# Dense stages of a two-block forward pass, from full fp32 products to three products of split high and low parts

## The reference

```python
def first_block(...):                      # DEPTH 2
    for i in range(2):
        sh1, sc1, g1, sh2, sc2, g2 = split(silu(c) @ ada_w[i] + ada_b[i], 6)  # 12 "rotations" of 1024 columns in all
        u = layer_norm(h) * (1 + sc1) + sh1
        if i == 0:
            uc = modulated layer_norm(ctx)                   # 256 context tokens
            p = u @ w_in                                     # 3072 columns: conv gates, q | k, v
            kv of the context = uc @ w_in[:, K0:]
            y = concat(conv_mixer, diff_attention) @ w_out_mix
        else:
            y = fourier_mix(u) @ w_out_fourier
        h = post_norm(h, g1 * y)
        h = post_norm(h, g2 * (relu(mod(h) @ mlp_w1)**2 @ mlp_w2))   # 1024 -> 4096 -> 1024
def second_block(...):
    h += fox_attention(rms_norm(h))        # fox_w_in 4 x 1024 columns, fox_w_out
    h += hier_moe(...)                     # 32 experts, 12 MB of weights for each pair of experts
    h += retention(rms_norm(h))            # ret_w_in 6 x 1024 columns, ret_w_out 2048 -> 1024
    h += hier_moe(...)
    return rms_norm(h)
```

## Time and profile before

| | us |
|---|---|
| median of 3 runs (2267.81 to 2272.15) | 2269.62 |
| the profiled execution, its own time | 2266.69 |
| its span, first to last instruction | 2264.9 |
| TensorE busy | 2138.2 |
| VectorE busy | 860.4 |
| ScalarE busy | 606.4 |

### The profile page before, as it was taken

How to read it: one execution, slowest core, us unless ns; L and a number is a source line. 1 busy time by engine, 2 the same in 40 slices (tenths; PEclk the granted TensorE clock), 3 DMA queues, 4 the chain that set the end, 5 groups by cost and what they waited for, 6 DMA issues and landing times.

```text
span 2264.9 us, 34188 instructions
## 1 busy us (share of the span) xinstructions
PE 2138.2 (94%) x13808; PEld 1421.8 (63%) x13809; DVE 860.4 (38%) x1536; ACT 606.4 (27%) x913; POOL 37.0 (2%) x38
## 2 busy tenths in 40 slices
PE   7998899999999997889999999989999899999998
PEld 5746777887888786754444444478887444444444
DVE  3765567653664664241111111156343111111112
ACT  1113366332673454211111111044411111111101
POOL 0000100000100200000000000000000000000000
PEclk9998999999999999989999999989998999999999
DMA  9950277822455255079999999825642799999994
GB/s 381 383 193 2 97 244 251 301 84 75 149 186 186 82 189 213 17 306 388 410 410 410 410 410 410 353 82 196 228 168 83 295 410 409 410 410 410 410 410 192
DMA packets 157222, 603.00 MB, mean 266 GB/s; under 512 B 10063, under 2 KB 10501, under 8 KB 157141
## 3 DMA queue, kind: packets, MB, share of 16 engines
q1 hardware_dynamic: 156544, 601.33, 69.4%
q0 software_dynamic: 320, 0.39, 0.1%
q10 hardware_dynamic: 276, 0.13, 0.0%
HBM read 600.73 MB, written 1.05 MB: 266 GB/s over the span
## 4 chain that ended last, share of the span: by engine, by line
PE 71%; SPq 10%; DMA 8%; ACT 4%; DVE 4%; issue 3%; DVEq 0%; ACTq 0%
PE bank L907 12%; PE bank L547 12%; SPq L421 9%; PE bank L525 7%; PE bank L919 6%; PE bank L548 6%; DMA expert_w<-in_expert_w_gu 5%; PE bank L891 4%; PE bank L584 4%; PE bank L938 4%; PE bank L566 3%; PE bank L674 1%; PE bank L673 1%; DMA u<-in_ada_w 1%; DMA dense_w<-in_ada_w 1%
## 5 line engine op out<-in xcount | busy, mean ns | idle before, releaser
L907 PE MATMUL bank<-expert_w,work 128*32 128x512 f32 (+1 forms) x4032 | 453.1, 597 | 26.8 <-issue 12.2
L907 PEld LDWEIGHTS bank<-expert_w,work 128*32 128x32 f32 (+1 forms) x4032 | 132.5, 111 | 345.9 <-issue 313.0
L395 DVE TENSOR_TENSOR w_low<-dense_w,w_high 128x2048 fp32r<-128x2048 f32 x96 | 219.4, 2291 | 172.5 <-ACT w_high L388 171.8
L388 ACT ACTIVATE w_high<-dense_w 128x2048 fp32r<-128x2048 f32 x104 | 197.5, 1911 | 265.2 <-DMA dense_w<-in_mlp_w 179.6
L919 PE MATMUL bank<-expert_w,work 128*32 128x512 f32 (+1 forms) x2016 | 226.4, 594 | 0.0
L1940 DVE TENSOR_TENSOR work<-work,bank 128x512 f32<-128x512 f32 x32 | 22.0, 688 | 410.1 <-ACT work L1324 410.1
L547 PE MATMUL bank<-hidden_pairs,w_high 128*128 128x512 f32 x496 | 174.5, 396 | 2.7 <-DVE expert_w L1452 2.7
L547 PE MATMUL bank<-u_pairs_mlp,w_high 128*128 128x512 f32 x448 | 164.5, 404 | 11.9 <-ACT u_pairs_mlp L1110 5.9
L919 PEld LDWEIGHTS bank<-expert_w,work 128*32 128x32 f32 (+1 forms) x2016 | 63.5, 110 | 144.4 <-issue 144.4
L547 PE MATMUL bank<-u_pairs,w_high 128*128 128x512 f32 x392 | 143.2, 403 | 6.4 <-DVE u_pairs L1434 5.4
L891 PEld LDWEIGHTS bank<-work 128*128 128x128 f32 x1088 | 125.9, 194 | 32.2 <-issue 32.1
(11 more groups left out here) (332 smaller groups left out, 2619.3 us busy)
## 6 DMA issues: line engine op xcount, KB each, us to landing
expert_w<-in_expert_w_gu SPq DMA_DIRECT2D x256, 1024.0 KB, 18.1
expert_w<-in_expert_w_down SPq DMA_DIRECT2D x128, 1024.0 KB, 16.7
dense_w<-in_mlp_w SPq DMA_DIRECT2D x64, 1024.0 KB, 5.2
dense_w<-in_ret_w_in SPq DMA_DIRECT2D x24, 1024.0 KB, 5.2
u<-in_ada_w SPq DMA_DIRECT2D x40, 512.0 KB, 6.3
work<-in_ada_w SPq DMA_DIRECT2D x40, 512.0 KB, 6.1
dense_w<-in_fox_w_in SPq DMA_DIRECT2D x16, 1024.0 KB, 5.2
dense_w<-in_w_in SPq DMA_DIRECT2D x12, 1024.0 KB, 8.3
```

Source lines behind the costliest of these rows:

```text
L388: nc.scalar.activation(w_high[:, at % RING], dense_w[:, at % RING], ACT.Copy, scale=scale).then_inc(S("w_high_ready"), 1)
L395: ins = nc.vector.tensor_tensor(w_low[:, at % RING], dense_w[:, at % RING], high, ALU.subtract)
L907: last = mm(free[half][cols, :], rows[:, k, cols], pieces[:, k, a, half * 512:(half + 1) * 512], start=k == 0, stop=k == KT - 1)
```

## The change

All dense stages use `by_rows` with split chunks and three products of 256 columns (keys and values, and the value blocks, 512): high by high, low weights by high, high weights by low. Each tile has one sum, evacuated by one engine (ScalarE for `w1`, with Relu, fox q, k and g, with Sigmoid for g, ret q, k and g, with Silu for g); `upper` and `sum_of` go. The activations of `w_in`, `mix`, `fourier`, `fox_out` and `ret_out` are split as well: high part on ScalarE, low part on VectorE, 256 columns at a time. For `w_in`, `fox_out` and `ret_out` there are only two places for high parts of chunks, so that a split waits until the chunk two before it is used. The context is loaded right behind x and normalised and turned before rotation 1; chunk (0, 0) of `w_in` is moved ahead of the last two ada chunks in the ring. Rotations 2 to 5 stay in the `w_in` stretch (pieces 0 to 31, two a chunk at first), 6 to 11 (48 pieces) are summed in the first MLP. The folds move: 6, 7 after the first MLP, 8, 9 after the next norm, 10, 11 after `post1_1`, in the place of warming products. GpSimd's loads wait for `mod_ready`. The last four pieces of the second expert stage's first pair are loaded after `ret_out` and not after the group norm's variance.

```diff
-                   ... ("ada_0", 4), ("z", 4), ("ada_1", 4), ("w_in", 8), ("zc", 4), ("w_in_1", 8) ...
+                   ... ("ada_0", 4), ("zc", 4), ("z", 4), ("ada_1", 4), ("w_in", 8), ("w_in_1", 8) ...
+        for table in (CHUNKS, SOURCE, LAST_TILE, USED, SPLIT_NO):
+            table.insert(6, table.pop(8))
+        HIGH_OF, WAS, holds = [], [], {}
+        for at, (name, i, j) in enumerate(CHUNKS):
+            where = {"w_in": (w_high, (4 * i + j) % 2), "fox_out": (w_high_fox, j % 2), "ret_out": (w_high_ret, (4 * i + j) % 2)}.get(
+                name, (w_high, at % RING))
+            key = (name if name in ("fox_out", "ret_out") else "", where[1])
+            HIGH_OF.append(where[0][:, where[1]])
+            WAS.append(holds.get(key) if name != "ada" and at - holds.get(key, 0) < RING else None)
...
         def split_high(act, at, scale=1.0):
             wait_chunk(act, at)
-            nc.scalar.activation(w_high[:, at % RING], dense_w[:, at % RING], ACT.Copy, scale=scale).then_inc(S("w_high_ready"), 1)
+            if WAS[at] is not None:
+                wait_used(act, WAS[at])
+            nc.scalar.activation(HIGH_OF[at], dense_w[:, at % RING], ACT.Copy, scale=scale).then_inc(S("w_high_ready"), 1)
...
+            sp.dma_start(ctx_tok, A["ctx"][0].rearrange("(t p) d -> p t d", p=P)).then_inc(S("in_ctx"), 16)
+            for at in range(chunk("w_in", 1, 0)):
                 load(at)
             sp.dma_start(const[:, N_FIRST:], A["consts"][:, N_FIRST:]).then_inc(S("in_const_rest"), 16)
+            for q in range(4):
+                load_ada(q)
+            q = 4
             for n, at in enumerate(range(chunk("w_in", 1, 0), chunk("w1_0", 0, 0))):
-                for q in range(4 * n, 4 * n + 4):
-                    load_ada(q)
                 load(at)
+                for _ in range(2 if n < 6 else 4):
+                    if q < 32:
+                        load_ada(q)
+                        q += 1
...
+            def columns(high, low):
+                def piece(out, n, k, w, w_rest, start, stop):
+                    c = slice(n * P, (n + 1) * P)
+                    mm(out[:, 0:SEQ], w[:, c], high[:, k, :], start=start, stop=False)
+                    mm(out[:, 0:SEQ], w_rest[:, c], high[:, k, :], start=False, stop=False)
+                    return mm(out[:, 0:SEQ], w[:, c], low[:, k, :], start=False, stop=stop)
+                return piece
...  # TensorE: the start
             ada(0)
-            pe.wait_ge(S("z_ready"), TT)
+            pe.wait_ge(S("z_ready"), 2 * TT)
+            turn("zc", ctx_tok)
             turn("z", z_tok)
             ada(1)
...  # VectorE: w_in, twelve steps
+            for step in range(3 * RING):
+                if 1 <= step < 3 * RING - 1:
+                    split("w_in", (step + 1) // RING, (step + 1) % RING)
+                if step == 0:
+                    ... modulate the context ...
+                if step == 1:
+                    ... low parts of the context ...
+                if step == 8:
+                    ... rope_q()
+                if step >= 8:
+                    conv(step - 8)
+                for q in range(2 * step, 2 * step + 2) if step < 8 else range(4 * step - 16, 4 * step - 12):
                     add_ada(q)
...  # VectorE: end of the first attention
+                if step == 4:
+                    split("mix", 0, 0)
+                    for n in range(4):
+                        low_of_cat(n)
+                    split("mix", 0, 1)
+                    low_of_cat(4)
+                    low_of_cat(5)
...  # ScalarE: ret_out
+            for n in range(2 * KT):
+                if n % 2 == 0:
+                    c = n // 2 + 1
+                    if c < 2 * RING:
+                        split("ret_out", c // RING, c % RING)
+                act.wait_ge(S("ret_gated"), n + 1)
+                fn(rgate_high[:, n, :], rgate[:, n, :], ACT.Copy).then_inc(S("rgate_high"), 1)
...  # VectorE: ret_out, for each head hd
+                for n in range(4 * hd, 4 * hd + 4):
+                    low_in_place(rgate_low[:, n, :], rgate[:, n, :], rgate_high[:, n, :], "rgate_high", n + 1, "rgate_low")
+                    if n % 2:
+                        c = n // 2 + 1
+                        if c < 2 * RING:
+                            split("ret_out", c // RING, c % RING)
...  # TensorE: ret_out
+                by_rows("ret_out", g, TILES["ret_out"], 8, columns(rgate_high[:, eight], rgate_low[:, eight]),
+                        lambda j: pe.wait_ge(S("rgate_low"), KT * g + 2 * j + 2), g == 0, g == 1)
```

More of the change, by code:

```diff
@@ L81 @@
 ADA_PE = 2
-ADA_HEAD = 8
+ADA_HEAD = 6
 HALVES = 4
+ADA_AT = {}
+for _x in range(24):
+    ADA_AT.setdefault(2 + 2 * _x // 3, []).append(32 + _x)
+for _x in range(24):
+    ADA_AT.setdefault(18 + 7 * _x // 12, []).append(56 + _x)
 ATTN = []
@@ new lines, in tokens, with piece @@
+            def tokens(high, low):
+                def piece(out, n, k, w, w_rest, start, stop):
+                    rows, c = slice(n // 2 * P, (n // 2 + 1) * P), slice((n % 2) * 512, (n % 2 + 1) * 512)
+                    mm(out[:, :], high[:, k, rows], w[:, c], start=start, stop=False)
+                    mm(out[:, :], high[:, k, rows], w_rest[:, c], start=False, stop=False)
+                    return mm(out[:, :], low[:, k, rows], w[:, c], start=False, stop=stop)
+                return piece
@@ L573, in pairs_of, with halves @@
+            def halves(where, k0=0):
+                x = pairs[where][:, k0:k0 + KT]
+                return x[:, :, HIGH, :], x[:, :, LOW, :]
             def pairs_of(name):
@@ L1211, in _ @@
                     deviation(sub_rstd[g % 2], T0 + diff_tile(g, 7), 1)
+                if step == 4:
+                    split("mix", 0, 1)
+                    high_of_head(0)
+                    high_of_head(1)
+                if step == 5:
+                    split("mix", 0, 2)
+                    high_of_head(2)
+            split("mix", 0, 3)
+            high_of_head(3)
             def mlp(l):
@@ L1306, in _ @@
                         copy_out(t, fpT[:, a, :], bank(t)[:, 0:384])
+                if step >= 2:
+                    high_of_gated(step - 2)
+            high_of_gated(FOX_HEADS // 2 - 1)
+            for j in (2, 3):
+                split("fox_out", 0, j)
             def experts(l):
@@ L1655, in _, with residual @@
                                            ALU.mult, ALU.mult).then_inc(S("sub_out"), 1)
-                if 1 <= step <= 3:
+                if 1 <= step <= 2:
                     for r in (2 * step, 2 * step + 1):
                         take_fold(T0 + ATTN.index(("f", r)), r)
-            def residual(name, l, gate, halves):
+                if step == 4:
+                    split("mix", 0, 0)
+                    for n in range(4):
+                        low_of_cat(n)
+                    split("mix", 0, 1)
+                    low_of_cat(4)
+                    low_of_cat(5)
+                if step == 5:
+                    split("mix", 0, 2)
+                    low_of_cat(6)
+            split("mix", 0, 3)
+            low_of_cat(7)
+            def residual(name, l, gate):
                 link(V.tensor_scalar(resid, h[:, :, :], ALPHA, None, ALU.mult))
@@ L1784, in _ @@
                     wait_tile(dve, t)
-                    dve.wait_ge(S("fox_gate"), g + 1)
+                    wait_evac(dve, TILES["fox_g"] + g)
                     evac(V.tensor_tensor(fgate[:, g, :], fgate[:, g, :], bank(t)[:, 0:SEQ], ALU.mult), t)
+                if step >= 2:
+                    low_of_gated(step - 2)
+            low_of_gated(FOX_HEADS // 2 - 1)
+            for j in (2, 3):
+                split("fox_out", 0, j)
             def add_to_h(name):
```

423 lines of the change are left out of this document (198 added, 225 removed).

## The result

The changed kernel takes 2287.1 us (median of 5 runs, 2284.3 to 2291.4), the kernel before 2270.0 beside it: ratio 1.0074, 95% interval 1.0058 to 1.0090. So it is slower by 17 us; 2260 was predicted, in a range that ended at 2282. The profiled execution has a span of 2286.8 against 2264.9, 21.9 more, at a mean granted clock of 0.965 against 0.974.

A forecast was written before the change was run, and what follows sets the result against it. Outside the expert stages TensorE's products were taken to bound the kernel, inside them the weights' transfers after some ten pairs. The terms summed to -7 us, so 2260 us was forecast, in a range of 2236 to 2282.

The forecast's parts named there:

- I take 0.116, so 0.348: Dense stages: a split product of 256 columns priced at 0.116 us, three in a row at 0.348.
- rival 3: Dense stages: three products of 256 cost 0.361, not 0.348, by a fixed 13 ns each; 2285 us; chance 17%.
- The two-in-a-row places: Sixteen tile closes in the earlier trace with two 256-column products in a row, 0.115 us each, taken as the price's model.
- The pair's remainder, 0.120: Upper bound for a 256-column product: pair of 0.347 less 0.2268 for 512 columns, so 0.361 us for three.
- w2 over 90.5 (pitch): Sign that would show the forecast wrong: the w2 stage taking over 90.5 us, by its product pitch.
- The start: Start and w_in: -5 us, bounds -14 to +3, with TensorE idle about 11 us before chunk (0, 2).
- Attention and `mix`: Attention and mix: 0 net, 5.3 us saved in products against a later mix start; bounds -4 to +3.
- First MLP -9.5: First MLP: -9.5 us, as one evacuation per tile takes VectorE out of the block boundaries; bounds -12 to +3.
- The fourth rival: First MLP: VectorE's queue at 90% and pieces ahead of chunks hold the loads; +12 on its term, 2272; chance 8%.
- Fourier, second MLP, `fox_in`, `ret_in`, `fox_out`: Later dense stages: Fourier -5.8 us, second MLP -1, fox_in and ret_in -0.5 each, fox_out -5.3.
- `ret_out` +17.5: ret_out: products give back 10.7 us, six gaps of 3.3 cost 20, lost clock 8; bounds +9 to +22.
- The rule on weight loads: TensorE: if loads overlapped products only across differing row groups, the change would lose some hundreds of us; given 1 in 100.

The follow-up runs named there:

- e3: Changed kernel with second-MLP product widths altered (384, 128 columns; values wrong), read for pitches alone: a triple of 384 columns takes 0.52 us, of 128 takes 0.33.
- e2: Changed kernel with w_in (0, 0) put back behind the last two ada rotation 1 chunks in the load order; ratio 1.0024 to the kernel before.
- e6: e2 with ada rotation 1 copies ahead of the split of w_in (0, 0), and the split of (0, 1) behind all x parts; ratio 1.0019 to before.
- e4: Changed kernel with w1 and w2 of both MLPs back as pairs of 512 and 256 columns; ratio 1.0129 to the kernel before.
- e1: Changed kernel with ScalarE's ret_out split of the next chunk behind the high parts of the current chunk's two tiles; ratio 1.0015 to the kernel before.
- e9: Changed kernel with ScalarE's and VectorE's ret_out lists reordered, e6's start orders, and VectorE's mix split and low parts made earlier; ratio 0.9860 to before.
- e8: Changed kernel with w2 of both MLPs and q, k blocks of fox_in and ret_in back as pairs; ratio 1.0100 to the kernel before.
- e12: e10 with w2 of both MLPs as pairs, w1 as triples; ratio 0.9815 to the kernel before.
- e10: e9 with TensorE making ada rotation 1 before turning context and x, and ScalarE's rotation 0 copies ahead of the context's squares; ratio 0.9821 to before.

## Why the prediction was wrong

- **The price of three products: the step that failed most.** "I take 0.116, so 0.348", and rival 3, at 17%, had 0.361. Measured 0.360. 0.012 on each of 1920 triples is 23 of the 29 us by which the span missed (-7 forecast, +21.9 measured); with that term alone put right the forecast would have been 2283. The two-in-a-row places looked like the very thing, but they stood between 512-column products, and there a single spacing is no price: over before's w2_1 a 256-column product starts 0.232 after a wide one and the next wide one 0.115 after it, 0.348 in sum. The pair's remainder, 0.120, came from a steady stream and was right. The 13 ns stand at 256, 384 (e3) and 512 columns, so the rival's mechanism holds at 256 columns. The prediction's own sign, "w2 over 90.5 (pitch)", came out at 92.3.
- **The start: the wait foreseen, its place in time not.** TensorE idle 11 us before (0, 2), by VectorE's split behind the additions: 11.37, q 0 added at 76.35 and the split after it. But (0, 2) starts at 81.2 where the forecast has 71.7, and that is 9.5 of the 10.3 us by which `w_in` ends late. (0, 0) was forecast at 47 and started at 51.9: the last ada chunk's products start at 43.0 for 41, and from there it took 9.0 us and not 6.5. Then two things had no term: VectorE's list holds z's banks (3.06 us in the first chunk), and after each wait products came at 0.21 for some us (granted clock 0.85 in the first two blocks). Keys and values took 43.9, as forecast. e2 and e6 show that the order of lists and slots made the wait before (0, 2), the one for z's banks and some 3 us of the late start.
- **Attention and `mix`:** `mix` released by VectorE as said; its start is 7.2 later than before where 1.6 earlier was forecast. The end of `w_in` alone was 10.3 late, the attention with its wait came out 1.5 better, without which the miss would have been larger.
- **First MLP -9.5:** measured -8.4. w1_0 gave 10.1, and e4 took it back, so the mechanism was right; w2_0 took 1.7 more with its triples. The fourth rival was not seen, although the transfers' share was 0.90 in w2_0 and VectorE busy 71 of 92 us.
- **Fourier, second MLP, `fox_in`, `ret_in`, `fox_out`:** each within about 1 us of its term once 0.012 for each of its triples is added. The fox attention took 1.9 more, as forecast.
- **`ret_out` +17.5:** measured +20.4. Six gaps, each released by a low part of the gate, 3.25 each for 3.3: the mechanism was right, and nearly the size. The clock took 10.2 for 8, the pitch 1.5. The heads' work does lie inside chunks, as the prediction says, but only while ScalarE's order makes the gaps; with that mended, 4.6 us of it stand in the way (e1).
- **The rule on weight loads** (the Trainium skill, TensorE: Matmul & The Clock Gate, What overlaps and what doesn't): the trace after speaks against it. The lines of the earlier trace rows list only the products. The loads, here those of w2_1 after, each of the full array, start with the product before their own, one every 0.120 us, and in the window of that stage TensorE and its load queue are both busy for all of 92.30 us:

```profile
748.63 0.19 PEld L555 LDWEIGHTS bank<-hidden_pairs,w_low 128*128 128x128 f32 x1
748.75 0.19 PEld L556 LDWEIGHTS bank<-hidden_pairs,w_high 128*128 128x128 f32 x1
```

  The same page's Back-to-back issue gap puts the spacing down to load and product together. The 13 ns and the 0.111 at 128 columns are compatible with that, but no run here parts the two, and the page's own figures, about 81 ns at 128 columns and 131 at 512, are not those measured here (111 and 227).

## What to carry to other kernels

Price a stream by a steady stream, over a whole period of it: 12 ns misread on 1920 triples decided the sign here. Where two engines feed a third through a ring of two, write both lists so that all that the next chunk needs stands ahead of the instruction that waits for the last one's use. The orders that e9 mends, in `ret_out`, at the start and before `mix`, cost this kernel 2.1%, three times what the change lost in all, and in `ret_out` the gaps took half as much again in clock (10.2 on 19.5 us).

## What the hardware showed

- In streams of split products the pitch is columns/2.4 GHz + 13 ns at 256, 384 and 512 columns, and 0.111 us at 128: if 0.111 is a floor, a product gets no cheaper below some 235 columns (an estimate from 0.111 and the 13 ns; no width between 128 and 256 was run).
- At the lower clock the 13 ns are gone. In `mix` after, just where the clock rises:

```profile
227.92 0.41 PE L555 MATMUL bank<-cat_high,w_low 128*128 128x256 f32 x1
228.14 0.41 PE L556 MATMUL bank<-cat_low,w_high 128*128 128x256 f32 x1
228.35 0.33 PE L554 MATMUL bank<-cat_high,w_high 128*128 128x256 f32 x1
...
228.75 0.28 PE L554 MATMUL bank<-cat_high,w_high 128*128 128x256 f32 x1
228.87 0.28 PE L555 MATMUL bank<-cat_high,w_low 128*128 128x256 f32 x1
```

  The pitch of 0.213 (0.21 to 0.22 in these rows) is 256 columns at 1.2 GHz; 0.120 is not half of it.
- A pair of 512 and 256 columns comes at 0.348 in some blocks (w2_1 of before and of e4) and at 0.353 in others (both w2 of e8 and e12) with TensorE never idle: 89.2 and 90.6 us for 256 pairs, the last product's end included. In e4's w2_1 a product behind a wide one starts nearly always 0.230 after it; in the dearer blocks the same spacing goes round in a cycle of three, 0.232, 0.241 and 0.236. The cause is open.
- TensorE's stretch from the end of `w_in` to `mix` has the same waits in e9 and e10 and takes 55.6 us at granted clock 0.88 and 59.4 at 0.80. Of the 8.4 us that e10's faster start had won, 3.7 are lost there.
